# Order and grouping of the Gram matmuls in a two-layer RWKV-7 and attention trunk

## The chip, the cores and the metric

The kernel runs on one core of one Trainium2 chip. The metric is the device time of one execution in microseconds (us). The kernel before takes 2891.14 us, the median of 3 runs (2888.48 to 2891.73).

## The reference

Two layers (`DEPTH` 2) over 256 tokens of width 2048. Each layer has a token mixer and a squared-ReLU MLP, each between two RMS norms. The mixer's 2048 columns are half RWKV-7 (16 heads of 64) and half causal attention (8 heads of 128). What matters here is the RWKV-7 recurrence:

```
def step(state, inp):
    r_t, w_t, k_t, v_t, a_t, b_t = inp
    sa = jnp.einsum('bhij,bhj->bhi', state, a_t)
    state = (state * w_t[:, :, None, :] + sa[..., None] * b_t[:, :, None, :]
             + v_t[..., None] * k_t[:, :, None, :])
    return state, jnp.einsum('bhij,bhj->bhi', state, r_t)
```

The kernel computes it in chunks of 64 tokens. For each head it needs the products of a and r with k and b inside a chunk (the Gram matrices); everything is float32.

## The kernel before

**Staging.** The program is written by hand engine by engine, with semaphores (`wait_ge`, `then_inc`) and no scheduler: each engine executes its instructions in the order of the code. SyncE fetches weights into four slots `raw`; ScalarE rounds a slot to a high part `whi` (L883), VectorE forms the rest `wlo` (L1128), and TensorE multiplies both with the activations `hT` or `mT`, whose own high and low parts stand side by side. One *tick* of this big matrix product is four matmuls: L537 (`whi`, 512 columns) and L538 (`wlo`, 256 columns) for each of two banks. In the last tick of a tile the order of the two is turned round (L538, L540).

**Pairs.** The mixer treats the heads in pairs: 8 per layer, 16 in all. Each pair goes once through `mixer` on TensorE, ScalarE and VectorE. Between the small matmuls of a pair TensorE executes ticks of the next pair's projection: `fill(m)` puts m ticks at that place, and at the end of the pair `fill(48)` whatever is left of its 48.

**The place of the change.** A pair has two heads, h = 0 on partitions 0 to 63 and h = 1 on partitions 64 to 127, and two halves of the tokens, u = 0 and 1, of 128 tokens each. A *unit* is one head with one half: `unit` = 2h + u. For each unit two matmuls are needed (L654), one with `ktl` (k) and one with `btl` (b) as the stationary operand, both with `AR` (a and r, 256 columns) moving. Both contract over the 64 partitions of the head. The products go to the left and the right half of the bank `mb[(unit + 2) % 4]`. VectorE multiplies each bank by a mask and writes it to `G` (L1252), as soon as the semaphore `gram_sum` says that the bank is full. When all four are done (`gram_ready`), TensorE turns a part of `G` (L661).

**What must be ready.** The banks are used by others before: `g_out` frees bank 2, `bonus_ready` bank 3, and `tm_ready` (ScalarE's copies L966) banks 0 and 1. VectorE signals `bonus_ready` at L1248; then it does one `wlo` (L1128, in `step(2)`) ahead of L1252.

In the trace every float32 matmul stands as two MATMUL records with a LDWEIGHTS (weight load) each, here called passes: the 16 L654 calls of two pairs are 32 records. The trace writes a matmul on 64 partitions as `64*128 64x256`, one on all 128 as `128*128`.

Of the kernel before, what the change touches and what calls it, by code (L numbers as in the profile page):

```python
# [41 lines left out]
HEAD = 64  # L42
# [65 lines left out]
def trunk(nc, consts, levels, x, norm_mix_pre, norm_mix_post, norm_mlp_pre, norm_mlp_post, w_in, w_in_vres,  # L108
          shift_mu, shift_mu_vres, decay_w0, decay_w2, iclr_a0, iclr_a2, vres_v0, vres_v2,
          gate_g2, k_k, k_a, r_k, lnx_gain, lnx_bias, w_out, w_up, w_down, out):  # L110
    with ExitStack() as ctx:
        def sb(name, shape, dt=F32):
            return ctx.enter_context(nc.sbuf_tensor("b_" + name, shape, dt))

        def sem(name):
            return ctx.enter_context(nc.semaphore(name))
# [3 lines left out]
        mb = [ctx.enter_context(nc.psum_tensor(f"mix_bank{i}", [P, 512], F32)) for i in range(4)]  # L120
# [28 lines left out]
        AR = sb("AR", [P, 2, 2, P])  # L149
        ktl = sb("ktl", [P, 2, P])  # L150
        btl = sb("btl", [P, 2, P])
# [69 lines left out]
        e = {n: sem("m_" + n) for n in names}  # L221
# [4 lines left out]
        start = {}  # L226
# [31 lines left out]
        def blocks(ap, lv, odd):  # L258

            dims = "p a" if len(ap.shape) == 3 else "p"  # L260
            ap = ap.rearrange(f"{dims} (n h b) -> {dims} n h b", h=2, b=1 << lv)
            return ap[:, :, :, odd, :] if dims == "p a" else ap[:, :, odd, :]

        def packed(ap, lv):

            dims = "p a" if len(ap.shape) == 3 else "p"
            return ap.rearrange(f"{dims} (n b) -> {dims} n b", b=1 << lv)
# [255 lines left out]
        def _(pe):  # L523
            mm, turned = nc.tensor.matmul, nc.tensor.transpose
# [67 lines left out]
            for b8 in range(8):  # L592
                bk = (bank + mb)[b8]
                pe.wait_ge(x_in[b8 // 4], 16)
                for q in range(2):
                    for u in range(2):
                        j = 2 * b8 + q
                        m = turned(bk[:, 256 * q + P * u:256 * q + P * u + P], yx[:, u, P * j:P * j + P], ident)
# [12 lines left out]
            def mixer(l, i, n, tiles, fill, more=True):  # L611


                V = n + 1
# [10 lines left out]
                if l:  # L625
                    mm(mb[3][:, 0:SEQ], lw[0:VRES, 2, :], lact[0:VRES, 2, :], start=True,
                       stop=True).then_inc(e["lora_v"], 1)
# [13 lines left out]
                for u in range(2):  # L641
                    for a, src in enumerate((btl[:, u, :], ktl[:, u, :], sh[:, 2, P * u:P * u + P])):
                        m = turned(mb[u][:, P * a:P * a + P], src, ident)
                    m.then_inc(e["turned"], 1)
                fill(2)

                for u in range(2):
                    pe.wait_ge(e["bonus_ready"] if u else e["g_out"], V)
                    pe.wait_ge(e["tm_ready"], 2 * n + u + 1)
                    for src, cols in ((ktl, slice(0, 256)), (btl, slice(256, 512))):  # L650
                        for h in range(2):
                            hs = slice(HEAD * h, HEAD * h + HEAD)
                            ar = AR[hs, u, :, :].rearrange("p a b -> p (a b)")
                            m = mm(mb[(2 * h + u + 2) % 4][:, cols], src[hs, u, :], ar, start=True, stop=True)  # L654
                            if src is btl:
                                m.then_inc(e["gram_sum"], 1)
                    fill(2)

                pe.wait_ge(e["gram_ready"], 4 * n + 4)
                for unit in range(4):  # L660
                    m = turned(mb[2][:, P * unit:P * unit + P], G[:, unit, 2, :], ident)  # L661
# [3 lines left out]
                for unit in range(4):  # L665
                    h, u = unit // 2, unit % 2
                    at = P * u + HEAD * h
                    m = mm(mb[3][:, at:at + HEAD], G[:, unit, 0, :], tm[:, u, 2, HEAD * h:HEAD * h + HEAD],
                           start=True, stop=True)
# [5 lines left out]
                for lv in range(1, LEVELS):  # L675
                    for w in range(2):
# [4 lines left out]
                        for unit in (2 * w, 2 * w + 1):  # L681
                            at = HEAD * (unit % 2)
                            m = mm(packed(mb[2 + w][:, at:at + HEAD], lv), G[:, unit, 2, :],  # L683
                                   blocks(TT[:, unit, 0, :], lv, 0), start=True, stop=True)
                        m.then_inc(e["x_sum"], 1)
                    fill(1)
                    for w in range(2):
                        pe.wait_ge(e["x_out"], 2 * (LEVELS - 1) * n + 2 * lv - 1 + w)
                        for unit in (2 * w, 2 * w + 1):
                            at = HEAD * (unit % 2)  # L690
                            if lv < LEVELS - 1:
                                mm(packed(mb[w][:, at:at + HEAD], lv), TT[:, unit, 1, :],  # L692
                                   blocks(X[:, unit, :], lv, 0), start=True, stop=True)
                            m = mm(packed(mb[w][:, P + at:P + at + HEAD], lv), X[:, unit, :],  # L694
                                   blocks(TT[:, unit, 1, :], lv, 1), start=True, stop=True)
# [4 lines left out]
                for c in range(NCH):  # L700
                    u, rows = c // 2, slice(CHUNK * (c % 2), CHUNK * (c % 2) + CHUNK)
                    if c:
                        pe.wait_ge(e["s_out"], (NCH - 1) * n + c)
                        mm(mb[0][rows, 0:P], AR[:, u, 0, rows], St[:, c, :], start=True,  # L704
                           stop=True).then_inc(e["r_sum"], 1)
# [4 lines left out]
                    for h in range(2):  # L710
                        hs = slice(HEAD * h, HEAD * h + HEAD)
                        m = mm(mb[0][rows, P + HEAD * h:P + HEAD * h + HEAD], TT[rows, 2 * h + u, 1, rows],  # L712
                               rhs[rows, u, hs], start=True, stop=True)
                    m.then_inc(e["u_sum"], 1)

                    m = mm(mb[3][rows, P * u:P * u + P], AR[:, u, 1, rows], St[:, c, :], start=True, stop=False,  # L716
                           skip_group_check=True)
# [7 lines left out]
                    if c < NCH - 1:  # L725
                        mm(mb[2][:, 0:P], tm[rows, u, 0, :], U[rows, u, :], start=False,  # L726
                           stop=True).then_inc(e["s_sum"], 1)
                    if c % 2:
                        for h in range(2):
                            hs = slice(HEAD * h, HEAD * h + HEAD)  # L730
                            at = P * u + HEAD * h
                            mm(mb[3][:, at:at + HEAD], G[:, 2 * h + u, 1, :], tm[:, u, 2, hs], start=False,
                               stop=False, skip_group_check=True)
                            m = mm(mb[3][:, at:at + HEAD], G[:, 2 * h + u, 3, :], U[:, u, hs], start=False,
                                   stop=True, skip_group_check=True)
                        m.then_inc(e["y_sum"], 1)
                    if c == 0:
# [4 lines left out]
                           stop=True).then_inc(e["score_sum"], 1)  # L742
# [4 lines left out]
                for u in range(2):  # L747
                    m = turned(mb[1][:, P * u:P * u + P], zt[:, 5, 1 + P * u:1 + P * u + P], ident)
# [4 lines left out]
                for j in range(3):  # L753
                    m = turned(mb[2][:, P * j:P * j + P], sm[:, P * j:P * j + P], ident)
# [11 lines left out]
                for u in range(2):  # L766
                    m = turned(mb[0][:, P * u:P * u + P], yn[:, u, :], ident)
# [3 lines left out]
            for l in range(DEPTH):  # L771
# [4 lines left out]
                if l == 0:  # L776

                    pe.wait_ge(prm_in, 16 * (8 + 8 + 2))
                    for j in range(2):
                        m = turned(mb[2][:, P * j:P * j + P], stage[:, j, :], ident)  # L780
                    m.then_inc(prm_turned, 1)
                if l:
# [6 lines left out]
                    for kt in range(KT):  # L789
                        cols = slice(VRES * kt, VRES * kt + P)  # L790
# [3 lines left out]
                        m = mm(bank[2][:, 0:SEQ], wlo[r][:, cols], hT[:, kt, 0, :], start=False, stop=False)  # L794
                        if kt:
                            m = mm(bank[2][:, :], whi[r][:, cols], pair, start=False, stop=kt == KT - 1)
# [12 lines left out]
                if l:  # L809
                    pe.wait_ge(e["pair_done"], PAIRS + 1)  # L810
                pe.wait_ge(inv_x, 2 * l + 1)
                key_norms(PAIRS * l)
                loop(pe, PAIRS - 1, lambda i: mixer(l, i, PAIRS * l + i, t + 4 + i * 6, filler(
                    lambda a, b: pair_ticks(a, b, k + 8, i * 3, t + 4 + i * 6), 48)))
                mixer(l, PAIRS - 1, PAIRS * l + PAIRS - 1, t + 46, filler(
                    lambda a, b: last_ticks(a, b, k + 92, t + 46), 40), False)

# [39 lines left out]
            for q in range(4):  # L857
# [4 lines left out]
                for u in range(2):  # L862
                    for j in range(4):
                        m = turned((bank + mb)[2 * q + u][:, P * j:P * j + P], xT[:, 4 * q + j, P * u:P * u + P],
                                   ident)
# [252 lines left out]
        def _(dve):  # L1118
# [71 lines left out]
            def mixer(l, i, n, tiles, step, finish, more=True):  # L1190


                V = n + 1
# [53 lines left out]
                    dve.wait_ge(e["v_ready"], V - PAIRS)  # L1247
                tt(t1[:, :], mb[3][:, SEQ:2 * SEQ], sh[:, 2, :], ALU.mult).then_inc(e["bonus_ready"], 1)  # L1248
                step(2)
                for at, unit in enumerate((0, 2, 1, 3)):  # L1250
                    dve.wait_ge(e["gram_sum"], 4 * n + at + 1)
                    tt(G[:, unit, :, :].rearrange("p a b -> p (a b)"), mb[(unit + 2) % 4][:, :],  # L1252
                       cst[:, C_GRAM:C_GRAM + 512], ALU.mult).then_inc(e["gram_ready"], 1)

# [49 lines left out]
                for c in range(NCH):  # L1304
                    u, rows = c // 2, slice(CHUNK * (c % 2), CHUNK * (c % 2) + CHUNK)
# [106 lines left out]
            for l in range(DEPTH):  # L1412
# [31 lines left out]
                def turn(i):  # L1444
                    def finish(g):

                        sums(t + 4 + 2 * g + i * 6, (2, 2, 0)[g + 1], place((1, 2, 0)[g + 1]))

                    def step(j):
                        if j == 0:  # L1450
                            dve.wait_ge(lo_done, k + 8 + LEAD + i * 12)
                        lo(k + 8 + j + LEAD, i * 3)
                    mixer(l, i, PAIRS * l + i, t + 4 + i * 6, step, finish)
# [7 lines left out]
                def step(j):  # L1461
                    if j == 0:
                        dve.wait_ge(lo_done, k + 92 + LEAD)
                    if j < 10:
                        lo(k + 92 + j + LEAD)
                mixer(l, PAIRS - 1, PAIRS * l + PAIRS - 1, t + 46, step, finish, False)
                k, t = start[l, "out"]
                hidden = lambda a: lambda b: yo[:, bass.ds(a + b, 1), :].rearrange("p a b -> p (a b)")
# [77 lines left out]
```

## Time and profile before

| | before |
|---|---|
| median of 3 runs | 2891.14 us |
| profiled execution, its own time | 2888.48 us |
| its span in the trace | 2886.5 us |
| TensorE (PE) busy | 2786.4 us, 97% |
| weight loads (PEld) busy | 2357.9 us, 82% |
| VectorE (DVE) busy | 1802.0 us, 62% |
| ScalarE (ACT) busy | 1282.4 us, 44% |
| GpSimd (POOL) busy | 327.2 us, 11% |
| mean granted clock of TensorE | 0.989 |

The span is the time from the first to the last instruction; the execution's own time is some 2 us longer. Matmuls overlap in the pipeline, so that the record of one lasts longer than its step: what it costs is read from the distance between the *starts* of neighbouring records.

### The profile page before, as it was taken

The numbers are of one execution on the slowest core, as the hardware profiler recorded it, in microseconds if no ns is written. First come the engines' busy times: TensorE is split into PE (matmuls) and PEld (weight loads), VectorE is DVE, ScalarE is ACT, GpSimd is POOL, SyncE is SP. The second block draws the span as 40 slices with busy tenths as digits, with TensorE's granted clock in tenths as the row PEclk, the third lists the DMA queues.
The fourth block names the chain that finished last, engine by engine and source line by source line (L and its number), as shares of the span: only waits on it lengthen the run. The fifth ranks groups of instructions, "written<-read, shape, count | busy, mean of one in ns | idle before, by whom it ended". The sixth has DMA issues, their size and how long they took to land.

```text
span 2886.5 us, 50956 instructions
## 1 busy us (share of the span) xinstructions
PE 2786.4 (97%) x16347; PEld 2357.9 (82%) x16347; DVE 1802.0 (62%) x3008; ACT 1282.4 (44%) x2144; POOL 327.2 (11%) x448
## 2 busy tenths in 40 slices
PE   7999999998999999999989999999989999999997
PEld 6888888886888888888768888887868888888886
DVE  6666666657655556556676666666576565565655
ACT  5443444444444444444453444443444444444443
POOL 3211111102000000000132222221120000000002
PEclk9999999999999999999999999999999999999998
DMA  6333333343655655556533333332435556555553
GB/s 185 99 89 107 92 96 96 95 139 112 189 189 177 194 182 185 191 177 190 155 105 104 96 93 93 97 97 89 153 116 184 190 179 194 183 182 190 181 188 110
DMA packets 518312, 415.90 MB, mean 144 GB/s; under 512 B 19422, under 2 KB 515696, under 8 KB 518256
## 3 DMA queue, kind: packets, MB, share of 16 engines
q1 hardware_dynamic: 515888, 412.88, 46.2%
q0 software_dynamic: 2368, 2.32, 0.3%
q8 instruction: 29, 0.48, 0.1%
q14 instruction: 27, 0.22, 0.0%
HBM read 413.03 MB, written 2.10 MB: 144 GB/s over the span
## 4 chain that ended last, share of the span: by engine, by line
PE 88%; DVE 8%; issue 1%; ACT 1%; POOL 0%; DMA 0%; DVEq 0%; ACTq 0%; POOLq 0%; SPq 0%
PE gemm_bank L537 45%; PE gemm_bank L538 24%; PE gemm_bank L540 3%; PE mix_bank L694 2%; PE mix_bank L683 2%; PE mix_bank L692 2%; DVE b_yo L1169 1%; PE mix_bank L654 1%; DVE b_yo L1152 1%; DVE b_rn L1201 1%; PE mix_bank L712 1%; PE mix_bank L716 1%; PE mix_bank L726 1%; PE mix_bank L722 1%; PE mix_bank L704 1%
## 5 line engine op out<-in xcount | busy, mean ns | idle before, releaser
L537 PE MATMUL gemm_bank<-b_hT,b_whi 128*128 128x512 f32 x3420 | 1269.6, 410 | 27.9 <-DVE b_hT L1149 14.4
L1128 DVE TENSOR_TENSOR b_wlo<-b_raw,b_whi 128x1024 fp32r<-128x1024 f32 x745 | 907.4, 1231 | 499.2 <-ACT b_whi L883 498.0
L883 ACT ACTIVATE b_whi<-b_raw 128x1024 fp32r<-128x1024 f32 x777 | 806.6, 1056 | 490.5 <-PE gemm_bank L538 482.8
L538 PE MATMUL gemm_bank<-b_hT,b_wlo 128*128 128x256 f32 x3648 | 1017.2, 283 | 0.0
L537 PE MATMUL gemm_bank<-b_mT,b_whi 128*128 128x512 f32 x2400 | 856.9, 400 | 1.5 <-DVE b_yo L1134 1.5
L537 PEld LDWEIGHTS gemm_bank<-b_hT,b_whi 128*128 128x128 f32 x3420 | 647.2, 189 | 192.2 <-issue 41.7
L538 PE MATMUL gemm_bank<-b_mT,b_wlo 128*128 128x256 f32 x2560 | 707.0, 281 | 0.0
L538 PEld LDWEIGHTS gemm_bank<-b_hT,b_wlo 128*128 128x128 f32 x3648 | 694.1, 190 | 14.8 <-issue 5.3
L537 PEld LDWEIGHTS gemm_bank<-b_mT,b_whi 128*128 128x128 f32 x2400 | 451.1, 188 | 110.3 <-issue 3.5
L538 PEld LDWEIGHTS gemm_bank<-b_mT,b_wlo 128*128 128x128 f32 x2560 | 484.1, 189 | 7.1
L891 ACT ACTIVATE b_xl<-gemm_bank 128x256 f32<-128x256 f32 x389 | 127.8, 381 | 301.6 <-PE gemm_bank L540 296.8
L478 POOL TENSOR_TENSOR b_gs<-b_gs,b_zt 128x256 f32<-128x256 f32 x56 | 38.1, 680 | 1499.0 <-ACT b_zt L917 1495.8
L993 ACT ACTIVATE b_U<-mix_bank 64x128 f32<-64x128 f32 x64 | 17.4, 271 | 239.9 <-PE mix_bank L712 239.9
L975 ACT ACTIVATE b_yo<-mix_bank 128x128 f32<-128x128 f32 x160 | 44.6, 279 | 166.1 <-PE mix_bank L683 166.1
L694 PE MATMUL mix_bank<-b_yo 128*128 128x64 f32 x640 | 114.9, 273 | 0.0
L1272 DVE COPY_PREDICATED b_yo<-b_lvl,mix_bank 128x128 f32<-128x128 uint8 x128 | 42.6, 333 | 104.6 <-PE mix_bank L694 104.6
L442 POOL TENSOR_TENSOR b_wlo<-b_raw,b_whi 128x1024 fp32r<-128x1024 f32 x32 | 76.1, 2380 | 188.7 <-DVE b_wlo L1128 172.4
L692 PE MATMUL mix_bank<-b_yo 128*128 128x64 f32 x512 | 95.3, 268 | 0.0
L694 PEld LDWEIGHTS mix_bank<-b_yo 128*128 128x128 f32 x640 | 93.4, 192 | 0.7
L1511 DVE TENSOR_TENSOR b_xl<-gemm_bank,b_xl 128x256 f32<-128x256 f32 x128 | 48.4, 419 | 71.6 <-ACT b_xl L891 71.6
L435 POOL TENSOR_TENSOR b_yo<-b_zt 128x256 f32<-128x256 f32 x32 | 20.8, 669 | 608.6 <-DVE b_zt L1134 608.6
L1493 DVE TENSOR_TENSOR b_AR<-gemm_bank,b_xl 128x256 f32<-128x256 f32 x128 | 48.4, 419 | 65.3 <-ACT b_xl L891 65.3
(229 smaller groups left out, 2562.7 us busy)
## 6 DMA issues: line engine op xcount, KB each, us to landing
b_raw<-in_w_up SPq DMA_DIRECT2D x256, 512.0 KB
b_raw<-in_w_down SPq DMA_DIRECT2D x256, 512.0 KB
b_raw<-in_w_in SPq DMA_DIRECT2D x384, 256.0 KB
b_raw<-in_w_out SPq DMA_DIRECT2D x48, 512.0 KB
b_raw<-in_w_out SPq DMA_DIRECT2D x32, 256.0 KB
b_raw<-in_w_in SPq DMA_DIRECT2D x8, 512.0 KB
b_yo<-in_x SPq DMA_DIRECT2D x2, 1024.0 KB, 6.8
out<-b_raw SPq DMA_DIRECT2D x8, 256.0 KB, 2.5
```

What stands on the lines that cost most here:

```text
L442: nc.gpsimd.tensor_tensor(wlo[at][:, :], raw[at][:, :, :].rearrange("p a b -> p (a b)"), whi[at][:, :].bitcast(F32), ALU.subtract).then_in ...
L537: mm(bank[b0 + b][:, :], whi[r][:, cols], pair, start=first, stop=False)
L538: m = mm(bank[b0 + b][:, 0:SEQ], wlo[r][:, cols], act[:, kt, 0, :], start=False, stop=False)
L540: m = mm(bank[b0 + b][:, :], whi[r][:, cols], pair, start=False, stop=True)
L683: m = mm(packed(mb[2 + w][:, at:at + HEAD], lv), G[:, unit, 2, :], blocks(TT[:, unit, 0, :], lv, 0), start=True, stop=True)
L692: mm(packed(mb[w][:, at:at + HEAD], lv), TT[:, unit, 1, :], blocks(X[:, unit, :], lv, 0), start=True, stop=True)
L694: m = mm(packed(mb[w][:, P + at:P + at + HEAD], lv), X[:, unit, :], blocks(TT[:, unit, 1, :], lv, 1), start=True, stop=True)
L883: f(whi[r][:, :], raw[r][:, :, :].rearrange("p a b -> p (a b)"), ACT.Copy).then_inc(hi_done, 1)
L891: f(xl[:, b, :], bank[b0 + b][:, SEQ:2 * SEQ], ACT.Copy).then_inc(half_out, 1)
L1128: tt(wlo[r][:, :], flat(raw[r][:, :, :]), whi[r][:, :].bitcast(F32), ALU.subtract).then_inc(lo_done, 1)
L1493: tt(hid(b), bank[2 * g + b][:, 0:SEQ], xl[:, b, :], ALU.add).then_inc(up_sum, 1)
L1511: tt(xl[:, b, :], bank[2 * g + b][:, 0:SEQ], xl[:, b, :], ALU.add).then_inc(down_sum, 1)
```

## The change

On TensorE the eight Gram matmuls of a pair stood in two blocks, one for each u, with both heads in a block and `fill(2)` behind each. Now they stand in four blocks, one for each unit, with one head in a block and `fill(1)` behind each. The order of the units goes from 0, 2, 1, 3 to 0, 1, 2, 3, on VectorE too. The waits move with the banks: units 2 and 3 alone wait for `tm_ready`. Nothing else is changed; the number of matmuls and of ticks is the same.

```
-                for u in range(2):
-                    pe.wait_ge(e["bonus_ready"] if u else e["g_out"], V)
-                    pe.wait_ge(e["tm_ready"], 2 * n + u + 1)
-                    for src, cols in ((ktl, slice(0, 256)), (btl, slice(256, 512))):
-                        for h in range(2):
-                            hs = slice(HEAD * h, HEAD * h + HEAD)
-                            ar = AR[hs, u, :, :].rearrange("p a b -> p (a b)")
-                            m = mm(mb[(2 * h + u + 2) % 4][:, cols], src[hs, u, :], ar, start=True, stop=True)
-                            if src is btl:
-                                m.then_inc(e["gram_sum"], 1)
-                    fill(2)
+                for unit in range(4):
+                    h, u = unit // 2, unit % 2
+                    b = mb[(unit + 2) % 4]
+                    if unit == 0:
+                        pe.wait_ge(e["g_out"], V)
+                    if unit == 1:
+                        pe.wait_ge(e["bonus_ready"], V)
+                    if unit >= 2:
+                        pe.wait_ge(e["tm_ready"], 2 * n + unit - 1)
+                    hs = slice(HEAD * h, HEAD * h + HEAD)
+                    ar = AR[hs, u, :, :].rearrange("p a b -> p (a b)")
+                    mm(b[:, 0:256], ktl[hs, u, :], ar, start=True, stop=True)
+                    mm(b[:, 256:512], btl[hs, u, :], ar, start=True, stop=True).then_inc(e["gram_sum"], 1)
+                    fill(1)
...
-                for at, unit in enumerate((0, 2, 1, 3)):
-                    dve.wait_ge(e["gram_sum"], 4 * n + at + 1)
+                for unit in range(4):
+                    dve.wait_ge(e["gram_sum"], 4 * n + unit + 1)
```

On TensorE, at the first Gram matmuls of a pair (L654 before; L658 and L659 are the same matmuls now; `mix_bank2` and `mix_bank0` are units 0 and 2, `mix_bank3` is unit 1; L537 and L538 are fill):

```order
-L649 ISA [waits m_g_out]
-L654 MATMUL mix_bank2<-b_AR,b_ktl 128x256 [waits m_tm_ready]
-L654 MATMUL mix_bank0<-b_AR,b_ktl 128x256
-L654 MATMUL mix_bank2<-b_AR,b_btl 128x256
-L654 MATMUL mix_bank0<-b_AR,b_btl 128x256
+L658 MATMUL mix_bank2<-b_AR,b_ktl 128x256 [waits m_g_out]
+L659 MATMUL mix_bank2<-b_AR,b_btl 128x256
 L537 MATMUL gemm_bank2<-b_hT,b_whi3 128x512
 L538 MATMUL gemm_bank2<-b_hT,b_wlo3 128x256
 L537 MATMUL gemm_bank3<-b_hT,b_whi3 128x512
 L538 MATMUL gemm_bank3<-b_hT,b_wlo3 128x256
+L658 MATMUL mix_bank3<-b_AR,b_ktl 128x256 [waits m_bonus_ready]
```

A block was the matmuls of two heads in turn; it is now the two matmuls of one head, and after one tick the next block follows.

On TensorE, from the last Gram matmul now to the turning of `G` (L664, L661 before):

```order
L658 MATMUL mix_bank1<-b_AR,b_ktl 128x256 [waits m_tm_ready]
L659 MATMUL mix_bank1<-b_AR,b_btl 128x256
L531 REGISTER_ALU [waits tile_out]
L537 MATMUL gemm_bank0<-b_hT,b_whi0 128x512 [waits lo_done,hi_done]
L538 MATMUL gemm_bank0<-b_hT,b_wlo0 128x256
L537 MATMUL gemm_bank1<-b_hT,b_whi0 128x512
L538 MATMUL gemm_bank1<-b_hT,b_wlo0 128x256
L664 MATMUL mix_bank2<-b_cst,b_yo 128x128 [waits m_gram_ready]
```

and the same stretch before:

```order
L654 MATMUL mix_bank3<-b_AR,b_btl 128x256
L654 MATMUL mix_bank1<-b_AR,b_btl 128x256
L538 MATMUL gemm_bank2<-b_hT,b_wlo3 128x256
L540 MATMUL gemm_bank2<-b_hT,b_whi3 128x512
L538 MATMUL gemm_bank3<-b_hT,b_wlo3 128x256
L540 MATMUL gemm_bank3<-b_hT,b_whi3 128x512
L531 REGISTER_ALU [waits tile_out]
L537 MATMUL gemm_bank0<-b_hT,b_whi0 128x512 [waits lo_done,hi_done]
L538 MATMUL gemm_bank0<-b_hT,b_wlo0 128x256
L537 MATMUL gemm_bank1<-b_hT,b_whi0 128x512
L538 MATMUL gemm_bank1<-b_hT,b_wlo0 128x256
L661 MATMUL mix_bank2<-b_cst,b_yo 128x128 [waits m_gram_ready]
```

Between the last Gram matmul and the turning stands one tick now, where two stood.

## Rows read from the trace of the kernel before

**Rows 1.** The page: shares of the chain that ended last, by engine.

```profile
PE 88%; DVE 8%; issue 1%; ACT 1%; POOL 0%; DMA 0%; DVEq 0%; ACTq 0%; POOLq 0%; SPq 0%
```

**Rows 2.** Pairs of either layer: us, busy PE PEld DVE ACT POOL, clock, DMA share, GB/s.

```profile
68.74:606.80 538.06, 524.92 (x3365) 434.16 (x3366) 355.23 (x748) 221.13 (x454) 86.08 (x135) 1.00 0.32 94
1499.07:2039.00 539.93, 530.99 (x3376) 435.76 (x3377) 359.19 (x756) 223.84 (x461) 116.55 (x154) 1.00 0.32 94
```

**Rows 3.** Waits of PE in one pair (202.73 to 270.06): us in total, times, longest.

```profile
PE mix_bank L633 <- DVE b_t L1215: 1.5, 1, 1.5
PE gemm_bank L537 <- DVE b_zt L1134: 0.3, 1, 0.3
```

**Rows 4.** PE around the first Gram block: start, duration (us), line, operands, count.

```profile
216.16 0.28 PE L538 MATMUL gemm_bank<-b_hT,b_wlo 128*128 128x256 f32 x1
216.37 0.70 PE L654 MATMUL mix_bank<-b_AR,b_ktl 64*128 64x256 f32 x4
216.91 0.60 PE L654 MATMUL mix_bank<-b_AR,b_btl 64*128 64x256 f32 x4
217.44 0.50 PE L537 MATMUL gemm_bank<-b_hT,b_whi 128*128 128x512 f32 x1
217.77 0.28 PE L538 MATMUL gemm_bank<-b_hT,b_wlo 128*128 128x256 f32 x1
217.89 0.40 PE L537 MATMUL gemm_bank<-b_hT,b_whi 128*128 128x512 f32 x1
218.12 0.28 PE L538 MATMUL gemm_bank<-b_hT,b_wlo 128*128 128x256 f32 x1
...
218.81 0.28 PE L538 MATMUL gemm_bank<-b_hT,b_wlo 128*128 128x256 f32 x1
```

**Rows 5.** The same place cut shorter: the first two passes of the first block.

```profile
216.37 0.49 PE L654 MATMUL mix_bank<-b_AR,b_ktl 64*128 64x256 f32 x2
```

**Rows 6.** PE from the end of the second block to the turning.

```profile
219.78 0.38 PE L654 MATMUL mix_bank<-b_AR,b_btl 64*128 64x256 f32 x2
220.09 0.39 PE L538 MATMUL gemm_bank<-b_hT,b_wlo 128*128 128x256 f32 x1
220.31 0.40 PE L540 MATMUL gemm_bank<-b_hT,b_whi 128*128 128x512 f32 x1
...
221.48 0.28 PE L538 MATMUL gemm_bank<-b_hT,b_wlo 128*128 128x256 f32 x1
221.60 0.60 PE L661 MATMUL mix_bank<-b_cst,b_yo 128*128 128x128 f32 x4
```

**Rows 7.** DVE in the same stretch, then PE's weight loads there.

```profile
216.16 0.41 DVE L1248 TENSOR_TENSOR b_t<-mix_bank,b_sh 128x256 f32<-128x256 f32 x1
216.60 1.23 DVE L1128 TENSOR_TENSOR b_wlo<-b_raw,b_whi 128x1024 fp32r<-128x1024 f32 x1
217.75 1.28 DVE L1252 TENSOR_TENSOR b_yo<-mix_bank,b_cst 128x512 f32<-128x512 f32 x2
220.19 1.29 DVE L1252 TENSOR_TENSOR b_yo<-mix_bank,b_cst 128x512 f32<-128x512 f32 x2 [1.16 <-PE mix_bank L654]
220.19 0.69 DVE L1252 TENSOR_TENSOR b_yo<-mix_bank,b_cst 128x512 f32<-128x512 f32 x1 [1.16 <-PE mix_bank L654]
...
221.25 0.19 PEld L538 LDWEIGHTS gemm_bank<-b_hT,b_wlo 128*128 128x128 f32 x1
221.53 0.43 PEld L661 LDWEIGHTS mix_bank<-b_cst,b_yo 128*128 128x128 f32 x4
```

**Rows 8.** PE at the first state chunk of the pair: matmuls on one group of 64 partitions.

```profile
243.97 0.44 PE L712 MATMUL mix_bank<-b_AKV,b_yo 64*64 64x64 f32 x4
...
244.70 0.49 PE L722 MATMUL mix_bank<-b_tm 64*128 64x128 f32 x2
245.12 0.50 PE L537 MATMUL gemm_bank<-b_hT,b_whi 128*128 128x512 f32 x1
```

**Rows 9.** Durations of L712's passes: count, then ns min/median/max, first and last start.

```profile
L712 PE MATMUL mix_bank<-b_AKV,b_yo x64: 217/218/268, 109.3 to 2013.5; 64*64 64x64 f32 x64
```

## The prediction

> **What bounds the kernel now.** I read the chain of waits first: 88% of it lies on TensorE (PE), 8% on VectorE (DVE) [rows 1]. Then the busy time by stretch: the sixteen pairs take 538.06 + 539.93 us of the 2886.5 us span. In the first layer PE is busy for 524.92 of 538.06 us, DVE for 355.23, ScalarE (ACT) for 221.13; the granted clock is 1.00 in both layers [rows 2]. A pair is therefore about 538.06 / 8 = 67.3 us of PE work. Then PE's waits inside one pair: 1.5 us for L1215 and 0.3 us for L1134 [rows 3]. Both waits stand ahead of the Gram matmuls in the program, and neither depends on them. So at the change PE has no wait that a longer block could fill: what the block grows by, the pair grows by, since the 48 ticks of fill have to be done anyway.
>
> Last the PE timeline at the Gram matmuls. The reader is to look at the starts. One tick is L537, L538, L537, L538, and in the plain stream L537 to L538 is 0.23 us (217.89 to 218.12) and L538 to the next 0.12 us (217.77 to 217.89) [rows 4]; a tick is 2 x (0.23 + 0.12) = 0.70 us.
>
> **What one Gram block costs now.** The last fill matmul ahead of it starts at 216.16, so the stream would have gone on at 216.16 + 0.12 = 216.28. The next fill matmul starts at 217.44, 1.16 us later, and its own step to the next is 0.33 us (217.44 to 217.77) where 0.23 is usual, 0.10 more. The block costs 1.16 + 0.10 = 1.26 us [rows 4]. The second block gives the same: 218.81 + 0.12 = 218.93 to 220.09 is 1.16, and 220.09 to 220.31 is 0.22 in place of 0.12, again 0.10 [rows 4, 6].
>
> What is in the 1.26 us? Eight passes, but they do not follow one another. The first two, cut out by themselves, start at 216.37 and last 0.49 us together [rows 5]: of two passes with a duration near 0.48 us each the second starts about 0.01 us behind the first. They are head 0 on partitions 0 to 63 and head 1 on 64 to 127. All eight go in such twos: four `ktl` passes end 0.70 us after 216.37, which with a last pass of 0.38 us puts the second two at 216.69; the `btl` passes start at 216.91 and end 0.60 us later, so that the last two start at 217.13 [rows 4, 6]. The steps are 0.32, 0.22, 0.22 and, out of the block, 0.31. Each of the four steps serves both heads. The rest is the way in and out: 0.09 us ahead of the block (216.28 to 216.37), 0.10 in its first step, 0.09 in its last and 0.10 in the first step of the fill, 0.38 us in all.
>
> **What the change makes of it.** *Four blocks for two.* Each new block holds one head: `ktl` and `btl`, four passes, all on the same 64 partitions, with a whole tick on 128 partitions behind them. There is no partner left to run beside them. Four passes one after the other take the same four steps as four twos did, and the ways in and out are paid per block. So a new block costs 1.26 us as the old one did, and there are four: 4 x 1.26 - 2 x 1.26 = 2.52 us more per pair, 16 x 2.52 = 40.3 us.
>
> That one head alone has the same steps and the same way out is an estimate; no row shows a single 64-partition block with 256 columns. The nearest row is L722, two passes on one group of 64 partitions with 128 columns. It starts at 244.70, lasts 0.49 us, and L537 follows at 245.12 [rows 8]. A full step of 256 columns is 0.22 us, so 128 columns less are 0.11 us less: its last pass lasts 0.38 - 0.11 = 0.27, and the two steps are 0.22 and 0.20. With 0.11 us more in each they would be 0.33 and 0.31: the first and the last step of the present block. From below: if alone a head paid no way in or out at all, a block would be 4 x 0.22 = 0.88 us, four of them 3.52, and the change 3.52 - 2.52 = 1.0 us per pair, 16 us in all. From above: if each weight load stood bare, three passes of each block (the first has its load bare already) would be longer by the 0.10 us of the first step, 4 x 3 x 0.10 x 16 = 19.2 us on top of the 40.3. Two things speak against the upper end. In the plain stream the load of every L538 and L537, on all 128 partitions, hides in steps of 0.12 and 0.23 [rows 4]. And L712's four passes on one group of 64 partitions, a load of 64 columns with each, lie in 0.44 us [rows 8]; the last is 0.22 long [rows 9], so the three steps ahead of it are 0.22 in all, 0.07 each, which leaves no room for bare loads. I take 1.26 us, the value that L722 supports.
>
> The Trainium skill, "TensorE: Matmul & The Clock Gate", section "Part 3: Packing small matmuls — row/col tiling", speaks against this change in the same sense: matmuls in different row groups run side by side, and a weight load overlaps a running matmul only when its row group is another one. By its first half the twos of the trace are what is lost, and the trace agrees. By its second half the loads of a block with one head would all be bare, which would make the sum that of the upper end; L712's loads are hidden on one and the same group, and so the trace does not bear out that half.
>
> *The turning of G.* Now DVE starts on the last two banks 0.41 us after the last pass of the block (219.78 to 220.19) and needs 1.29 us for both; PE's weight load for L661 starts 0.05 us after that (221.48 to 221.53), and its matmul 0.12 us after the matmul ahead of it, which is the plain step [rows 6, 7]. Two ticks of fill just cover two banks. After the change only the last bank is left when the last block ends: 0.41 + 0.69 + 0.05 = 1.15 us from the last pass to the load [rows 6, 7]. The cover is one tick: 0.31 to the fill, then 0.33 + 0.12 + 0.23 + 0.12 = 0.80, so that the matmul is due at 1.11 us and its load, which in a plain stream starts together with the matmul ahead (L538: 221.25, one step of 0.23 ahead of 221.48), at 0.99 us. The load is 1.15 - 0.99 = 0.16 us late. I take 0.15 us per pair, 16 x 0.15 = 2.4 us. The bounds are 0 and 0.4 us (a bare load and a way into an idle array on top, 0.10 each), 0 to 6 us.
>
> *The other edits cost nothing.* Unit 0 no longer waits for `tm_ready` and PE did not wait for it: there is no such wait [rows 3]. Unit 1 now comes after one block and one tick in place of one block and two: 1.07 + 0.80 + 0.09, about 1.96 us after 216.37 instead of 2.65 [rows 4]. Its bank is freed by L1248, which ends at 216.16 + 0.41 = 216.57, 0.2 us after the first pass [rows 7], so 1.7 us of cover remain. DVE has one L1128 between L1248 and the first bank and comes to L1252 at 217.75 [rows 7]; blocks then come every 1.96 us and a bank takes it 0.69, so it is free each time. ACT and the weight slots get their signals one or two blocks later, at most 2.5 us, on engines that are idle for a third and more of the stretch [rows 2]. The ticks are the same 48, and what follows the turning in a pair waits on it in the same way as before; it all moves back together.
>
> **The sum.** 40.3 + 2.4 = 42.7 us. The profiled execution of before took 2888.48 us, its span 2886.5 and 2.0 around it; with the change it would take 2931.2 and its span 2929.2. The median of the three runs of before is 2.7 us above that execution, which makes 2933.8 for a median. I put the time at 2933.
>
> **Rivals.**
>
> *Bare loads.* The upper end above: every load on the same 64 partitions waits for the pass ahead. 42.7 + 19.2 = 62 us more, 2953 us. L712 and the plain stream, where a tick on 128 partitions has no bare load, speak against it; for it speaks only that no such block with 256 columns is in the trace. 6%.
>
> *Cheap single blocks.* The way in and out is mostly the cost of having two heads at once, so that a single head has little of it: 16 to 28 us more, 2907 to 2919 us. L722's steps speak against it. 5%.
>
> *Not slower: a block halves with its heads.* The ends of the records are modelled; if in truth the two heads' passes took turns in the array, a lone pass would take half a step, 0.11 us, and if half of the ways in and out belonged to either head, a lone block would be 4 x 0.11 + 0.19 = 0.63 us. Four of them are 2.52 us, what the two blocks cost now, and the time is 2891 us, with the wait at the turning 2894. For it: `wlo`'s 256 columns do take a step of 0.12 [rows 4]. Against it: L722, a lone pass of half the columns, needs 0.20 to 0.22 [rows 8]. It decides when a lone block costs less than 0.63 + 5.8 / 64 = 0.72 us. 2%.
>
> *Clock.* Blocks with half the array at work could let the granted clock fall to 1.2 GHz somewhere after them. The granted clock is 1.00 in all sixteen pairs, blocks of 64 partitions among them [rows 2]. It would double the steps of a pair for some microseconds: 16 x 1 to 3 us on top, 2950 to 2980. 2%.
>
> **How the numbers follow.** The forecast, four blocks at 1.26 us and a short wait, has 85%. Its own range is 2926 to 2941: 38 to 46 us more than a median of 2888.5 to 2894. To hold the time 8 times in 10 I reach a little to both neighbours: 2925 to 2944. A difference of 0.2%, 5.8 us, is about what a measurement of this kernel can tell from no change. Slower by more than that are the forecast, bare loads, cheap blocks and clock, 0.97; within 0.2% is the third rival, 0.02; faster 0.01, for what no case here covers.
>
> **What would show it.** In the profile of the changed kernel: the Gram matmuls (L658, L659) start singly, not in twos 0.01 us apart, four to a block, with steps of 0.32, 0.22, 0.22 and 0.31 us; their 256 records stay 256, but blocks are 64. The block with its tick repeats every 1.96 us. A pair is 70.0 us long where it was 67.3. DVE waits ahead of each bank but the first, and L664's weight load comes about 0.05 us after the end of the last L1255 and some 0.15 us late. The stretches outside the pairs keep their length. The prediction is wrong if two passes of one head start less than 0.2 us apart, if a block costs other than 1.2 to 1.35 us, or if PE's other waits in a pair shrink by what the blocks add.

## The result and the profile after

The changed kernel takes 2931.12 us (median of 4 runs, 2930.35 to 2931.97); the kernel before 2890.51 us (4 runs, 2888.48 to 2891.73). The ratio is 1.0141, with a 95% interval of 1.0127 to 1.0155: 40.6 us slower. Forecast were 2933 us, and 42.7 us more.

The page after, busy time and shares of the chain; it reads as before, a span of 2927.5 us with 2826.8 us of PE [rows 1]:

```profile
PE 2826.8 (97%) x16347; PEld 2377.9 (81%) x16347; DVE 1805.9 (62%) x3008; ACT 1282.0 (44%) x2144; POOL 327.2 (11%) x448
...
PE 89%; DVE 8%; issue 1%; ACT 1%; POOL 0%; DMA 0%; DVEq 0%; ACTq 0%; POOLq 0%; SPq 0%
```

Where the time went: the first weight loads (L622) of the eight pairs of the first layer, here of before (count, ns min/median/max, first and last start in us), and then of after:

```profile
L622 PEld LDWEIGHTS mix_bank<-b_lact,b_lw x16: 183/184/187, 68.7 to 539.6; 64*128 64x128 f32 x16
```

```profile
L622 PEld LDWEIGHTS mix_bank<-b_lact,b_lw x16: 182/184/186, 68.6 to 557.7; 64*128 64x128 f32 x16
```

From the first to the eighth pair it was 470.9 us and is 489.1: 18.2 us for seven pairs, 2.60 us each. In the second layer (1499.0 to 1971.6, now 1519.3 to 2009.9) it is 18.0 us, 2.57 each. Sixteen pairs make 41.4 us, as much as the whole span grew (2927.5 - 2886.5 = 41.0, within 0.4 us); so the rest of the run did not grow.

PE at the first Gram block of the third pair after, which answers to [rows 4, 5]:

```profile
221.28 0.28 PE L538 MATMUL gemm_bank<-b_hT,b_wlo 128*128 128x256 f32 x1
221.49 0.70 PE L658 MATMUL mix_bank<-b_AR,b_ktl 64*128 64x256 f32 x2
222.02 0.59 PE L659 MATMUL mix_bank<-b_AR,b_btl 64*128 64x256 f32 x2
222.54 0.50 PE L537 MATMUL gemm_bank<-b_hT,b_whi 128*128 128x512 f32 x1
222.88 0.28 PE L538 MATMUL gemm_bank<-b_hT,b_wlo 128*128 128x256 f32 x1
222.99 0.40 PE L537 MATMUL gemm_bank<-b_hT,b_whi 128*128 128x512 f32 x1
223.23 0.28 PE L538 MATMUL gemm_bank<-b_hT,b_wlo 128*128 128x256 f32 x1
223.44 0.70 PE L658 MATMUL mix_bank<-b_AR,b_ktl 64*128 64x256 f32 x2
```

The counts are 2 where they were 4, and the durations are the same 0.70 and 0.6 us: two passes now take what four took. The block costs (222.54 - 221.28 - 0.12) + (222.88 - 222.54 - 0.23) = 1.14 + 0.11 = 1.25 us, and the next begins 1.95 us after the first: 1.25 for the block and 0.70 for its tick.

Then the turning: PE, its weight loads and DVE after the last block, which answers to [rows 6, 7]:

```profile
228.40 0.51 PE L537 MATMUL gemm_bank<-b_hT,b_whi 128*128 128x512 f32 x1
...
229.10 0.28 PE L538 MATMUL gemm_bank<-b_hT,b_wlo 128*128 128x256 f32 x1
229.26 0.66 PE L664 MATMUL mix_bank<-b_cst,b_yo 128*128 128x128 f32 x4
229.67 0.48 PE L537 MATMUL gemm_bank<-b_hT,b_whi 128*128 128x512 f32 x1
```

```profile
228.51 0.69 DVE L1255 TENSOR_TENSOR b_yo<-mix_bank,b_cst 128x512 f32<-128x512 f32 x1 [1.26 <-PE mix_bank L659]
...
229.25 0.42 PEld L664 LDWEIGHTS mix_bank<-b_cst,b_yo 128*128 128x128 f32 x4 [0.19 <-DVE b_yo L1255]
```

DVE ends at 229.20; the load starts at 229.25, where the plain stream would have had it at 229.10, with L538. The waits of the whole run say the same (us in total, times, longest). DVE waits for three of every four banks, which costs nothing by itself, and the weight load of the turning waits in each pair.

```profile
DVE b_yo L1255 <- PE mix_bank L659: 55.5, 48, 1.3
...
PEld mix_bank L664 <- DVE b_yo L1255: 3.3, 16, 0.2
```

### The profile page after: what moved, and what is told of

Read it like the earlier page. It is cut to its first block, busy times and chain, and to the rows that moved or that the text cites. A ratio compares the mean times of both kernels' runs of the same rounds, so it can differ in the third digit from the quotient of the medians.

```text
span 2927.5 us, 50952 instructions
## 1 busy us (share of the span) xinstructions
PE 2826.8 (97%) x16347; PEld 2377.9 (81%) x16347; DVE 1805.9 (62%) x3008; ACT 1282.0 (44%) x2144; POOL 327.2 (11%) x448
## 4 chain that ended last, share of the span: by engine, by line
PE 89%; DVE 8%; issue 1%; ACT 1%; POOL 0%; DMA 0%; DVEq 0%; ACTq 0%; POOLq 0%; SPq 0%
PE gemm_bank L537 45%; PE gemm_bank L538 24%; PE gemm_bank L540 3%; PE mix_bank L697 2%; PE mix_bank L686 2%; PE mix_bank L695 2%; PE mix_bank L658 1%; DVE b_yo L1172 1%; DVE b_rn L1204 1%; PE mix_bank L659 1%; PE mix_bank L715 1%; PE mix_bank L719 1%; DVE b_yo L1155 1%; PE mix_bank L729 1%; PE mix_bank L725 1%
## 5 line engine op out<-in xcount | busy, mean ns | idle before, releaser
L537 PE MATMUL gemm_bank<-b_hT,b_whi 128*128 128x512 f32 x3420 | 1273.2, 411 | 28.1 <-DVE b_hT L1152 14.4
L538 PE MATMUL gemm_bank<-b_hT,b_wlo 128*128 128x256 f32 x3648 | 1016.8, 283 | 0.0
L537 PE MATMUL gemm_bank<-b_mT,b_whi 128*128 128x512 f32 x2400 | 856.7, 400 | 1.7 <-DVE b_yo L1137 1.7
L537 PEld LDWEIGHTS gemm_bank<-b_hT,b_whi 128*128 128x128 f32 x3420 | 647.0, 189 | 201.4 <-issue 51.7
L538 PE MATMUL gemm_bank<-b_mT,b_wlo 128*128 128x256 f32 x2560 | 706.8, 281 | 0.0
L538 PEld LDWEIGHTS gemm_bank<-b_hT,b_wlo 128*128 128x128 f32 x3648 | 693.7, 190 | 14.2 <-issue 5.3
L537 PEld LDWEIGHTS gemm_bank<-b_mT,b_whi 128*128 128x128 f32 x2400 | 451.0, 188 | 110.6 <-issue 4.3
L538 PEld LDWEIGHTS gemm_bank<-b_mT,b_wlo 128*128 128x128 f32 x2560 | 483.8, 189 | 7.1
```

The source lines that it names most:

```text
L537: mm(bank[b0 + b][:, :], whi[r][:, cols], pair, start=first, stop=False)
L538: m = mm(bank[b0 + b][:, 0:SEQ], wlo[r][:, cols], act[:, kt, 0, :], start=False, stop=False)
```

## The experiments

The ratios below are to the kernel before, which ran beside each (2890.35 to 2891.06 us).

**e1: two blocks, one head each.** Both units of a head stand in one block, all waits ahead of it; VectorE takes the banks in the same order.

```
-                for u in range(2):
-                    pe.wait_ge(e["bonus_ready"] if u else e["g_out"], V)
-                    pe.wait_ge(e["tm_ready"], 2 * n + u + 1)
...
+                for h in range(2):
+                    pe.wait_ge(e["tm_ready"], 2 * n + 2)
+                    pe.wait_ge(e["g_out"], V)
+                    pe.wait_ge(e["bonus_ready"], V)
...
+                    for u in range(2):
...
+                        mm(b[:, 0:256], ktl[hs, u, :], ar, ...)
+                        mm(b[:, 256:512], btl[hs, u, :], ar, ...)
                     fill(2)
```

> Two blocks per pair as in the kernel before, but each holds the two units of one head: eight passes in a row on the same 64 partitions, two ticks behind each block. The theory (a block is a fixed way in and out of 0.40 us plus 0.216 us for each step, loads hidden on the same partitions, and a lone pass takes a whole step): eight steps for four, 4 x 0.216 x 2 = 1.73 us per pair, 27.6 us in all, 2890.5 + 27.6 = 2918. Rival A (weight loads on the same partitions stand bare once passes follow one another for long): steps of 0.32, 14 x 0.10 more per pair, 2940. Rival B (the cost of the change is per block, not per lost partner): no change, 2891.

Measured: 2924.67 us, ratio 1.012 (1.0103 to 1.0136), 34.3 us more, 6.7 above the theory. PE in the third pair:

```profile
221.13 0.28 PE L538 MATMUL gemm_bank<-b_hT,b_wlo 128*128 128x256 f32 x1
221.62 0.67 PE L655 MATMUL mix_bank<-b_AR,b_ktl 64*128 64x256 f32 x2 [0.21 <-DVE b_t L1248]
222.12 0.59 PE L656 MATMUL mix_bank<-b_AR,b_btl 64*128 64x256 f32 x2
222.56 0.59 PE L655 MATMUL mix_bank<-b_AR,b_ktl 64*128 64x256 f32 x2
222.99 0.59 PE L656 MATMUL mix_bank<-b_AR,b_btl 64*128 64x256 f32 x2
223.51 0.51 PE L537 MATMUL gemm_bank<-b_hT,b_whi 128*128 128x512 f32 x1
```

Each further two passes take 0.43 us, 0.216 a step: the loads stay hidden over eight passes on the same 64 partitions. The block's first pass, however, is late by a wait for L1248 that my edit brought in; over the run PE waits 8.1 us for it, 16 times. That is enough for the 6.7, and e5 tests it.

**e5: the same, each wait at its own unit.** `g_out` and `bonus_ready` stand ahead of head 0's first and second unit, `tm_ready` ahead of head 1's.

> The kernel of e1 (two blocks, one head each, eight passes in a row on the same partitions), with each unit's wait directly ahead of it instead of all ahead of the block. In e1 the first block began 0.49 us (first layer) and 1.09 us (second layer) after its neighbour where 0.21 is usual, because it waited for bonus_ready, which this order moves away. The theory: only the four lone steps more are left, 4 x 0.216 x 2 x 16 = 27.6 us, 2918. Rival (e1's 34 us are the price of long blocks on one head, not of the wait): 2925 again.

Measured: 2921.07 us (2917.33 to 2923.48), ratio 1.0107 (1.0092 to 1.0123), 30.7 us more, an interval of some 27 to 36. The first block begins 0.21 us after its neighbour again, and no wait for L1248 is left in the trace:

```profile
218.91 0.28 PE L538 MATMUL gemm_bank<-b_hT,b_wlo 128*128 128x256 f32 x1
219.12 0.70 PE L656 MATMUL mix_bank<-b_AR,b_ktl 64*128 64x256 f32 x2
```

In the profiled run, which took 2917.33 us, the pairs of the first layer are 68.99 us apart on average where they were 67.27 (L622, 68.0 to 550.9): 1.72 us more, where the theory has 1.73; in the second layer it is 1.70. So the theory holds in this trace. The median is 3.7 us above that run. The median of the kernel before is 1.9 us above its own profiled run; for the other 1.8 us I have no line, and they are within the interval.

**e2: four blocks, heads side by side.**

```
                             if src is btl:
                                 m.then_inc(e["gram_sum"], 1)
-                    fill(2)
+                        fill(2 if u and src is btl else 1)
```

with `fill(1)` for `fill(2)` ahead of the blocks.

> Four blocks per pair as in the changed kernel, but both heads stay side by side: a block holds the two ktl matmuls or the two btl matmuls of a half, four passes in twos. One tick is taken from ahead of the blocks and put behind the last, so that the turning stays covered by two ticks. The theory: two steps a block, 0.40 + 0.43 = 0.83 us, four of them 3.32 for 2.52, 0.80 us per pair, 12.8 us in all, 2903. Rival B (the cost is per block): 2931. Rival C (the ways in and out are hidden or small, only the lost partner costs): 2891.

Measured: 2901.71 us, ratio 1.0042 (1.0028 to 1.0057), 11.4 us more against 12.8. A block is one `ktl` line of count 4:

```profile
217.68 0.28 PE L538 MATMUL gemm_bank<-b_hT,b_wlo 128*128 128x256 f32 x1
217.89 0.70 PE L654 MATMUL mix_bank<-b_AR,b_ktl 64*128 64x256 f32 x4
218.52 0.50 PE L537 MATMUL gemm_bank<-b_hT,b_whi 128*128 128x512 f32 x1
```

So the change's 40 us are two things: 11 to 13 us for two more ways in and out per pair, and 28 to 31 us for the partner.

**e3: two blocks, the two heads one after the other in each.**

```
-                    for src, cols in ((ktl, slice(0, 256)), (btl, slice(256, 512))):
-                        for h in range(2):
...
+                    for h in range(2):
...
+                        mm(b[:, 0:256], ktl[hs, u, :], ar, ...)
+                        mm(b[:, 256:512], btl[hs, u, :], ar, ...)
```

> Two blocks per pair with the same eight matmul passes each as before and the same ticks; only the order inside a block differs: first both matmuls of head 0, then both of head 1. The theory with passes started in program order: only head 0's last pass and head 1's first can stand side by side, seven steps for four, 3 x 0.216 x 2 = 1.30 us per pair, 20.7 us in all, 2911. Rival D (the queue starts head 1's passes beside head 0's by itself, order does not matter): 2891. Rival E (a change of partitions drains the array, no overlap at all): eight steps and more, 2918 or above.

Measured: 2889.78 us, ratio 0.9999 (0.9989 to 1.0009): no change. The theory's clause on program order fell, and rival D stands. The trace shows it:

```profile
217.49 0.28 PE L538 MATMUL gemm_bank<-b_hT,b_wlo 128*128 128x256 f32 x1
217.70 0.71 PE L654 MATMUL mix_bank<-b_AR,b_ktl 64*128 64x256 f32 x4
218.23 0.60 PE L655 MATMUL mix_bank<-b_AR,b_btl 64*128 64x256 f32 x4
218.77 0.49 PE L537 MATMUL gemm_bank<-b_hT,b_whi 128*128 128x512 f32 x1
```

All four `ktl` passes lie in 0.71 us and start ahead of the four `btl` passes, though head 0's `btl` stands ahead of head 1's `ktl` in the program.

**e7: one block, all of head 0 and then all of head 1.** The four units in the order 0 to 3 in one block, all waits ahead, with `fill(3)` ahead of the block and behind it.

> One block of sixteen passes in program order unit 0, 1, 2, 3: first all eight of head 0, then all eight of head 1. One tick is moved ahead of it so that its waits are over; three follow. e3 showed that head 1's passes are started beside head 0's although two matmuls of head 0 stand ahead of them in the program. If the queue does that over eight passes too: eight steps, as e6, 2884 to 2887. If it reaches only over the four of e3: some 12 steps, 0.40 + 12 x 0.216 - 2.52 = 0.47 us per pair, 2898. If nothing of it is left: 15 or 16 steps, 0.40 + 15.5 x 0.216 - 2.52 = 1.23 us per pair, 2910.

Measured: 2901.06 us, ratio 1.004 (1.0024 to 1.0055), 10.7 us more: the middle case, forecast at 7.5.

```profile
218.32 0.28 PE L538 MATMUL gemm_bank<-b_hT,b_wlo 128*128 128x256 f32 x1
218.53 0.70 PE L655 MATMUL mix_bank<-b_AR,b_ktl 64*128 64x256 f32 x2
219.07 0.59 PE L656 MATMUL mix_bank<-b_AR,b_btl 64*128 64x256 f32 x2
219.50 0.70 PE L655 MATMUL mix_bank<-b_AR,b_ktl 64*128 64x256 f32 x4
219.93 0.70 PE L656 MATMUL mix_bank<-b_AR,b_btl 64*128 64x256 f32 x4
220.47 0.59 PE L655 MATMUL mix_bank<-b_AR,b_ktl 64*128 64x256 f32 x2
220.90 0.59 PE L656 MATMUL mix_bank<-b_AR,b_btl 64*128 64x256 f32 x2
221.42 0.50 PE L537 MATMUL gemm_bank<-b_hT,b_whi 128*128 128x512 f32 x1
221.76 0.28 PE L538 MATMUL gemm_bank<-b_hT,b_wlo 128*128 128x256 f32 x1
```

Four passes alone, four joined by four of the other head, four alone: twelve steps. Head 1 started when three passes of head 0 were still ahead of it in the program, as in e3, and not earlier. The first joined four last 0.70 us, as at the start of a block, and not 0.60: head 1's first pass has the longer first step once more, 0.10 us that the forecast left out. The whole block costs (221.42 - 218.32 - 0.12) + (221.76 - 221.42 - 0.23) = 3.09 us, 0.59 more than two blocks of 1.25, 9.4 us in all; the last 1.3 us are within the interval.

**e8: the changed kernel with its blocks in the order 0, 2, 1, 3.** Only the order of the lone blocks is changed, on VectorE too, each with its own wait, so that neighbours are of different heads.

> The changed kernel with its four blocks in the order of units 0, 2, 1, 3, as VectorE had it before, so that neighbouring blocks are of different heads with one tick on all partitions between. The theory: a tick on 128 partitions uses both heads' rows, so nothing can be started beside it or over it; the order of lone blocks does not matter, 2931. Rival (the queue that puts heads side by side in e3 reaches over a tick as well): blocks join, 2911 or less.

Measured: 2932.24 us, ratio 1.0142 (1.0126 to 1.0157), as the changed kernel. A tick on all 128 partitions keeps the blocks apart.

**e4: two ticks behind the last lone block.** One of them is taken from ahead of the first.

```
                     m.then_inc(e["turned"], 1)
-                fill(2)
+                fill(1)
...
-                    fill(1)
+                    fill(1 + unit // 3)
```

> The changed kernel with one tick of fill taken from ahead of the first Gram block and put behind the last, so that two ticks cover the last bank before the turning. The theory: only the wait at the turning goes, 0.10 to 0.15 us per pair, 1.6 to 2.4 us in all against the changed kernel, 2929; the load of L664 follows its neighbour by the plain step. Rival (the wait only moves to the next thing that PE needs from DVE): 2931, the wait found at a later line.

Measured: 2929.53 us (2927.32 to 2931.88), ratio 1.0139 (1.0122 to 1.0156). The 1.6 us below the changed kernel is less than runs differ, so the time alone shows nothing. The trace does; PE's matmul and load at the turning:

```profile
228.79 0.28 PE L538 MATMUL gemm_bank<-b_hT,b_wlo 128*128 128x256 f32 x1
228.91 0.60 PE L664 MATMUL mix_bank<-b_cst,b_yo 128*128 128x128 f32 x4
229.26 0.48 PE L537 MATMUL gemm_bank<-b_hT,b_whi 128*128 128x512 f32 x1
```

```profile
228.79 0.47 PEld L664 LDWEIGHTS mix_bank<-b_cst,b_yo 128*128 128x128 f32 x4
```

The load starts with L538, and from L538 to the fill behind the turning it is 0.47 us where the changed kernel has 0.57 (229.10 to 229.67). The wait costs 0.10 us in this pair. The others agree: from the first pair to the eighth it is 488.3 us (L622, 68.5 to 556.8) where the changed kernel has 489.1, and 489.9 where it has 490.6 in the second layer, 0.11 and 0.10 us a pair. That is 1.6 us in all.

**e6: one block for both halves.** In the kernel before, `fill(4)` behind the loop over u in place of `fill(2)` in it.

> The kernel before with both halves in one block of sixteen passes in twos, and the four ticks behind it. The theory: one way in and out less, 0.40 us per pair, 16 x 0.40 = 6.4 us less than before, 2884, faster than both kernels. Rival F (the second half's wait for bonus_ready, which now stands 1.06 us after the block's start instead of 2.65, holds the block): part or all of it is given back, 2886 to 2891. Rival G (a longer block on two heads delays G for DVE): the turning waits, 2891 or more.

Measured: 2886.53 us (11 runs), ratio 0.9984 (0.9975 to 0.9993): faster by 0.16%, though not by the 6.4 us. The pairs of the first layer are 66.90 us apart on average where they were 67.27, 0.37 us less. Two pairs of the run pay some of it back, as PE's timeline shows in the ninth pair:

```profile
1512.06 0.60 PE L654 MATMUL mix_bank<-b_AR,b_btl 64*128 64x256 f32 x4
1513.80 0.70 PE L654 MATMUL mix_bank<-b_AR,b_ktl 64*128 64x256 f32 x4 [1.15 <-DVE b_t L1248]
```

That is rival F: PE waits 2.3 us in all for L1248, in two pairs; 16 x 0.37 - 2.3 = 3.6 us are left, close to the measured 3.8.

**e9: the same with one tick moved from behind the block to ahead of it** (`fill(3)` and `fill(3)`).

> The kernel of e6 (one block of sixteen passes in twos) with one of the four ticks moved from behind the block to ahead of it. In e6 two of the sixteen pairs lost 1.1 us each in the middle of the block, where the second half waited for bonus_ready (L1248, itself behind GpSimd's v in the second layer). The theory: 0.70 us more cover ends or nearly ends that wait, the full 16 x 0.38 = 6 us of the way in and out are left, 2884.5 against 2890.4 before. Rival (three ticks no longer cover DVE's four banks before the turning): a wait at L661 and 2887 or more.

Measured: 2883.57 us (8 runs, 2881.29 to 2885.66), ratio 0.9975 (0.9965 to 0.9986), 7.5 us less than before. No wait for L1248 is left in its trace, and none at the turning. It is faster than both kernels.

**e10: e9 with two ticks moved from the end of a pair to its start** (`fill(9)` for `fill(7)`).

> The kernel of e9 with two of the ticks that stand at the end of a pair moved to its start, ahead of the wait for t1 (L633), which costs PE 1.5 us in the pairs of the first layer, and so ahead of the wait for btl (L643) in the second. The theory: the ticks have to be done anyway, so 1.4 us of work per pair fills 1.2 to 1.5 us of waits, 10 to 18 us less, 2870. Rival (the ticks at the end of the pair cover DVE's last work there, and the next pair starts later by as much): 2884. Rival (weights for the ticks are not split yet at that place): 2884 or more, a wait at L537 for L1128.

Measured: 2918.13 us, ratio 1.0098 (1.0082 to 1.0113), 35 us slower than e9. The theory failed (2870), and the second rival was right in its cause, though it gave no size beyond "2884 or more"; PE's waits (us in total, times, longest):

```profile
PE gemm_bank L537 <- DVE b_wlo L1128: 46.4, 34, 2.8
...
PE mix_bank L633 <- DVE b_t L1215: 3.5, 6, 0.7
```

The wait for L1215 did fall, from 10.3 us in e9, but PE now waits for `wlo` at the ticks, 46.4 us where e9 has 7.3. DVE splits those weights behind the very work for which the ticks were to be a cover: in the third pair it forms `wlo` only from 218.20 us, after `btl` (L1242, from 217.87), and PE waits 1.5 us for it there.

## Why the prediction was right

*What bounds.* That a pair is PE's work end to end held: pairs grew by 2.59 us, the blocks by 4 x 1.25 - 2 x 1.25 = 2.50 and the turning by 0.10, and no wait of PE shrank by more than 0.2 us over the run. Inside the third pair the two waits of [rows 3] are the same 1.5 and 0.3 us after. A pair was to be 70.0 us long and is 69.9 in the first layer, 70.1 in the second.

*Four blocks for two.* Forecast 1.26 us a block, measured 1.25 (the blocks of the kernel before are 1.25 too if taken from the distance between their starts, 219.02 - 216.37, less two ticks of 0.70); forecast steps of 0.32, 0.22, 0.22 and 0.31, and measured the same. The sum of 40.3 us is 40.0 with the measured blocks. e2 and e5 separate its parts, which the prediction had as 0.38 us of ways and 0.22 us a step: 11.4 us measured for two ways more per pair (12.8), and 30.7 for four lone steps more (27.6); together 42, with intervals wide enough for the 40.

*Bare loads.* This rival was wrong. In a row of eight passes on one group of 64 partitions each step is 0.216 us (e1), where bare loads would make it 0.32. The Trainium skill, "TensorE: Matmul & The Clock Gate", section "Part 3: Packing small matmuls — row/col tiling", lists an overlap of load and matmul only between different row groups; by it the lone blocks would have cost 19 us more, and the measurement decides against it.

One more rival has to be ruled out: that a step of 0.216 us is itself a bare load and a shorter pass. Starts alone speak against it. The two passes of L722, with 128 columns on one group of 64 partitions, take 0.42 us up to the next fill (244.70 to 245.12) [rows 8]; the first and the last step of a lone block, with 256 columns, take 0.32 + 0.31 = 0.63. So 128 columns are some 0.105 us of a pass and 256 are 0.21, the whole step, and no room is left for a load in it. This is an estimate from two kinds of matmul; no run changed the columns alone.

*Cheap or halved blocks, and the clock.* Wrong too: the lone block costs 1.25 us, far from 0.72. What spoke for the halved block, that `wlo`'s 256 columns take a step of 0.12, compares unlike things. The tiles of a tick (`whi`, `wlo`, `hT`, `mT`) are declared float32r in the kernel, and each of their matmuls is one record, though the trace prints f32 for it too; two records stand only for a matmul on plain float32 tiles. A plain float32 pass with 256 columns takes the same 0.22 us on all 128 partitions: after, the two passes of L609 start at 1650.87 and the next matmul at 1651.31. The granted clock is 1.00 in the pairs after (us, busy PE PEld DVE ACT POOL, clock, DMA share, GB/s), as before [rows 2]:

```profile
68.65:627.57 558.92, 546.06 (x3365) 444.40 (x3366) 357.04 (x748) 221.14 (x454) 86.04 (x135) 1.00 0.31 90
1519.14:2079.64 560.50, 551.32 (x3375) 445.59 (x3376) 360.86 (x756) 224.01 (x461) 116.58 (x154) 1.00 0.31 90
```

*The turning.* Here a term was mis-sized: 0.15 us a pair was forecast, 2.4 us in all. The load is indeed 0.15 us late, but e4 against the changed kernel shows that this costs 0.10 us, 1.6 in all. The step that failed is that a late load was put down in full. In the kernel before the load was already 0.05 us late (221.53, with L538 at 221.48) without moving its matmul [rows 6, 7], which the prediction had in its rows and did not count.

*What was free.* Right: PE has no wait for `tm_ready`, `g_out` or L1248 after. e1 and e6 show that this rested on where the waits stand. A wait for `bonus_ready` ahead of the first unit costs 8 us, and in the middle of a joined block 2.3.

The forecast of 42.7 us more is 2.1 above the measured 40.6: 0.3 of it are the blocks, 0.8 the turning, and the last 1.0 is less than the runs of one kernel differ. One slip without effect: the chances of the cases slower by more than 0.2% (0.85, 0.06, 0.05 and 0.02) add up to 0.98, not 0.97.

## What to carry to other kernels

Where matmuls of half the partitions each stand side by side, separating them cost here the full time of each, in rows of four passes as in rows of eight (the change and e5); count steps (distances between starts), not records. Going from matmuls on all partitions to matmuls on half of them and back cost some 0.4 us here each time (e2, e6), so such work belongs in one block, placed so that its waits are over before it. Work that covers a wait needs its own inputs at that place: ask who makes them before moving it (e10).

## What the runs showed of the hardware

The program order of the two heads' matmuls inside a block did not matter with four passes of each head (e3, ratio 0.9999), and with eight of each it mattered in part (e7, twelve steps for sixteen passes where eight would do). Matmul records of head 1 start ahead of up to three passes of head 0 that stand before them in the program. I had expected matmuls to start in program order, as the expectation of e3 has it; that each engine executes its instructions in the order of the code, as the staging of the kernel before is described, does not hold for these. Whether it is a number of matmuls, of instructions or of something else that limits this was not tried. Across a tick on all partitions nothing joins (e8).
